# A decoder step with routed experts: where GpSimd's gathers stand among its scatters

## The reference, cut to what matters

```python
rows = jnp.zeros((R, D), x.dtype).at[dest].set(x[tok])        # rows grouped by expert, in blocks
def expert_block(args):
    xb, e = args
    return swiglu(xb, w_g[e], w_u[e], w_d[e])                 # (silu(x Wg) * (x Wu)) Wd, 1024 -> 256 -> 1024
y = y_rows[dest] * gate.reshape(A)[order][:, None]            # weighted
routed = jax.ops.segment_sum(y, tok, num_segments=N)          # and added back to each token's row
```

## Time and profile before

| what | value |
|---|---|
| median of 3 runs | 2397.28 us (2396.0 to 2401.74) |
| the profiled execution, device time | 2394.25 us |
| its span, first to last instruction | 2392.5 us |
| busy share of the span: PE, DVE, ACT, POOL | 92%, 58%, 49%, 37% |
| mean granted clock of TensorE | 0.957 of full |
| expert loop, first to last `part_copied` of a rest | about 1396 to 2338 us |

### The profile page before, as it was taken

The page is one execution under the profiler, slowest core; times in us unless marked ns, Lnnn a source line. Parts: engine busy times, 40 slices in busy tenths (PEclk is TensorE's granted clock), DMA queues, the critical chain, the costliest instruction groups (busy, mean ns, idle before and its releaser), DMA issues. The chain is left out here.

```text
span 2392.5 us, 48606 instructions
## 1 busy us (share of the span) xinstructions
PE 2201.8 (92%) x18304; PEld 1717.5 (72%) x18304; DVE 1376.5 (58%) x2494; ACT 1177.2 (49%) x1931; POOL 892.6 (37%) x1019
## 2 busy tenths in 40 slices
PE   8999899799877799999999899999999999999990
PEld 7566666679866699996546477777777777777760
DVE  4644355422186545543664377777767777777765
ACT  3366433322143333331211167777777777777762
POOL 0133411000042000000244256767666767766653
PEclk9999899899978799999999899999999999999995
DMA  4000332311000555441133389999999999999844
GB/s 153 14 1 1 131 123 103 124 57 45 35 7 2 171 185 177 151 135 64 36 121 123 106 294 313 314 315 309 317 303 309 311 315 309 318 308 315 280 145 168
DMA packets 97313, 419.15 MB, mean 175 GB/s; under 512 B 21782, under 2 KB 29606, under 8 KB 67238
## 3 DMA queue, kind: packets, MB, share of 16 engines
q1 hardware_dynamic: 63494, 320.46, 37.0%
q0 software_dynamic: 33424, 96.15, 15.0%
q10 hardware_dynamic: 288, 1.05, 0.1%
HBM read 374.46 MB, written 63.09 MB: 183 GB/s over the span
## 5 line engine op out<-in xcount | busy, mean ns | idle before, releaser
L2630 DVE TENSOR_TENSOR split<-mix,split 128x2048 fp32r<-128x2048 f32 x140 | 321.5, 2298 | 250.9 <-ACT split L2553 215.7
L2481 PE MATMUL banks<-split 128*128 128x512 f32 x1680 | 403.1, 395 | 0.0
L2481 PEld LDWEIGHTS banks<-split 128*128 128x128 f32 x1680 | 310.5, 188 | 76.7 <-issue 14.1
L2405 POOL DMA_INDIRECT y_rows<-mix x140 | 292.6, 2090 | 162.6 <-ACT mix L2581 113.1
L2553 ACT CAST split<-mix 128x2048 fp32r<-128x2048 f32 x140 | 266.2, 1903 | 0.0
L2388 POOL DMA_INDIRECT hq<-x_rows,mix x136 | 218.6, 1607 | 85.0 <-POOL mix L2380 59.5
L1992 POOL DMA_INDIRECT slot_table<-route x72 | 68.7, 953 | 474.9 <-DVE route L2197 455.7
L2502 PE MATMUL banks<-split 128*128 128x512 f32 x840 | 211.7, 401 | 5.8 <-DVE split L2659 5.8
L1787 PE MATMUL banks<-merge_split 128*128 128x368 f32 x1152 | 203.0, 333 | 2.3 <-DVE merge_split L1850 2.3
L1787 PEld LDWEIGHTS banks<-merge_split 128*128 128x128 f32 x1152 | 196.8, 189 | 2.5 <-DVE merge_split L1850 2.5
L2502 PEld LDWEIGHTS banks<-split 128*128 128x128 f32 x840 | 154.2, 190 | 35.5 <-issue 5.9
(11 more groups left out here) (380 smaller groups left out, 3943.6 us busy)
## 6 DMA issues: line engine op xcount, KB each, us to landing
mix<-in_w_exp_down SPq DMA_DIRECT2D x70, 1024.0 KB
merge_rest<-in_w_merge SPq DMA_DIRECT2D x47, 768.0 KB, 4.3
mla<-in_w_exp_gate SPq DMA_DIRECT2D x35, 1024.0 KB
mla<-in_w_exp_up SPq DMA_DIRECT2D x35, 1024.0 KB
mix<-in_w_exp_gate SPq DMA_DIRECT2D x35, 1024.0 KB
mix<-in_w_exp_up SPq DMA_DIRECT2D x35, 1024.0 KB
inputs_rest<-in_x_tiles SPq DMA_DIRECT2D x9, 512.0 KB, 4.3
mla<-in_x_cols SPq DMA_DIRECT2D x12, 368.0 KB, 10.4
```

What stands on the lines that cost most here:

```text
L2405: pool.indirect_dma_start(out=S.y_dram, in_=y[0:p, s, hf], in_offset=None, compute_op=ALU.add, out_offset=bass.IndirectOffsetOnAxis(ap=si[ ...
L2481: ins = pe.matmul(PS[:, MBANK].rearrange("p (j n) -> p j n", j=2), xr[:, a, k], wr[:, s, GATE:UP + 1, b, DEXP * k:DEXP * (k + 1)], start=( ...
L2630: dve.tensor_tensor(parts(s, j)[:, LO], raw[s][j], parts(s, j)[:, HI].bitcast(F32), ALU.subtract).then_inc(parted[j], 1)
```

## The change

In POOL's step for a block, the call that issues the block's two scatters now stands ahead of the gathers of the third block ahead.

```diff
@@ stage_experts, gpsimd, body @@
                     factors(*ahead(s, it, 2), at[s + 2])
+                scatter(s, it, at[s], first)
                 if s < gathers:
                     pool.wait_ge(xr_full, 2 * (n + 2))
                     pool.sem_inc(passed, 1)
                     gather(*ahead(s, it, 3), at[s + 3])
-                scatter(s, it, at[s], first)
```

## The result

The changed kernel takes 3165.68 us (median of 4 runs, 3162.96 to 3166.49), the one before 2396.64 in the same comparison: 1.32 times as long, 95% interval 1.3173 to 1.3226. That is 769 us more, or 11.48 for each of the 67 blocks whose gathers moved. The forecast was 3034.

The account below looks back on a forecast made before the run. PE was taken as the bound, busy 199.26 of 200 us. Period 13.6 + 7.24 + 2.4 = 23.2 against 13.69: 67 x (23.24 - 13.69) = 640 us, added to 2394.25, gave 3034 us; range 2860 to 3200.

Parts of the forecast that it names:

- each mark named at the end of the prediction: L2449 idle 6 to 7 us until the gather's DMA, period 22 to 24, issue ending T + 11.7, clock under 1.00.
- T: The end of ACT's last copy of a block, which releases POOL; the prediction counts all times in a block from it.
- The landing: Gathered rows land 1.9 us after POOL's issue ends, so PE's turns (transposes of them) start at T + 13.6, not T + 6.4.
- the drain: DMA engines working off a block's 13.0 us of transfers from about T, empty before T + 14, the gather last.
- From the turns to T: PE's transposes of gathered rows, down product, its rest and ACT's copy, up to the next T: 7.24 us at full clock.
- The lower clock: After PE's gap of 7 us, 5.4 us at 1.2 of 2.4 GHz following each restart, costing 2.4 us a block.
- The price by the Trainium skill: Skill page's 1.67 us throttled per tile, half of it lost; gave a period of 21.7 and a total near 2930 us.
- Clock up throughout: Rival: PE's clock stays up or recovers at once despite the gap; 479 us added, 2873 us; chance 0.12.
- Quick POOL: Rival: POOL's calls run quicker once collisions shift; gathers landed at T + 9.0, period 16.2, 2565 us; chance 0.04.
- The rival with the clock down over the whole ring: PE's clock stays low from T through scatter, gather, turns and down to next T; period 25.6, 3192 us; chance 0.12.
- Not slower: Rival: scatters land sooner and free `y` sooner, so POOL, ACT and PE never wait; 3.4 us won, 2391 us; chance 0.02.
- no effect: Rival: the change only rotates POOL's cyclic list of calls; 2394 us; chance 0.02.

Follow-up runs that it names:

- clock held: Changed kernel plus 76 transposes of the identity on PE ahead of its wait for the gathered rows, in every block but the first two: 2990.27 us.
- the run with the short DVE operation: Changed kernel with DVE's subtraction of the gate and up weights cut from 2048 to 256 columns: 3146.88 us.
- light weights besides: Changed kernel with each weight load cut from 2048 to 512 columns and DVE's gate and up subtraction cut to 256: 2964.13 us.
- the kernel with the adds behind and light weights: Changed kernel with only the two scatter DMAs put back behind the gathers and each weight load cut from 2048 to 512 columns: 2547.93 us.

## Why the prediction was right, and where its sizes were off

The mechanism held: each mark named at the end of the prediction showed up, with three sizes beyond it. The wait of L2449 is 8.6 us in the mean and not 6 to 7, the period 25.2 and not 22 to 24, the DMA share 0.51 and not near 0.6.

- **What moves, how often, and POOL's issue.** 67 blocks; scatters from T + 0.9, picks held by DVE's subtraction, issue ending at T + 11.8 against 11.7. As worked out. The factors' new place is free, shown by its own run.
- **The landing** is the term that was mis-sized: 1.9 after the issue, turns at T + 13.6. It measured 3.5 and T + 15.3 early in the loop; over 67 blocks the mean start is T + 15.1. Two reasons. The lower bound came from a scatter that landed 1.35 after its issue, and a gather alone takes 2.7. That scatter was a poor stand-in: its packets in the trace are 23 rows, and the next block's scatter, with 8 rows, took 1.34, where a gather of the loop moves some 130. Nor were the DMA engines idle beside it: the heading of the rows says that no weights are loaded there, but weight packets ran to 2317.9, 0.8 us before its issue ended. No run varied the number of rows. The other reason: the drain was placed right (the windows above are full to T + 14), and no landing was added behind it. 1.5 us x 67 = 100 us.
- **From the turns to T, and the clock.** 7.24 at the full clock: 7.2 with the clock held. The lower clock: 2.4 expected for 5.4 us of it after the restart; 4.7 us of it in the block shown, up to 8.0 in others, and 2.6 by the run that held it. The period's second part is 10.0 in the mean instead of 9.6: 0.4 x 67 = 27 us. With the landing's 100 that is the 132 us between 3034 and 3166, but for 5.
- **The price by the Trainium skill.** Its figure (the Trainium skill, "TensorE: Matmul & The Clock Gate", section "HAM oscillation — how this bites in real kernels") gave an estimate of 0.84 us a block for a cold restart, and a total of 2930. This case does not agree: the clock-held run says 2.6 us a block.
- **The rivals.** Clock up throughout is refuted by the clock row. Quick POOL was made in the run with the short DVE operation: its issue ends at T + 8.9, and the turns still start at T + 15.4, since the drain holds them. With light weights besides, they start at T + 12.2 and not at T + 9.0. The rival with the clock down over the whole ring, 3192, is nearest in time for the wrong reason: the clock came back 4.7 us after the restart in the block shown, before the next T. That the range reached to 3200 was owed to this rival. The forecast with the latest landing that it allowed, T + 14.4, comes to 3088 only, so that the measured 3166 lies in the range is in part luck. Not slower and no effect are refuted by the time.

## What to carry to other kernels

Before moving an issue on an in-order engine, write down which event its new predecessor waits for, and follow it round: if it comes back to the moved transfer's consumer, the period becomes the sum of that ring and every busy share falls. Price a landing from a transfer of its own kind and size, and look at the drain of what shares the engines as a second bound. Where PE gets a gap of several us in each pass, add its lower clock after each restart.

## What the runs showed of the hardware

In the kernel with the adds behind and light weights PE waited 0.8 to 2.8 us in 63 blocks, and in 29 of them the granted clock fell to 0.50 for a stretch after PE was busy again (at 1543.5 us in the rows above, full clock in the gap itself); I had expected that of gaps of 4 us and more. The length of the gap alone did not decide: the clock fell after one of 1.3 us and stayed up after one of 2.4. Of the 26 gaps of 1.6 us and more 18 were followed by it, of the 37 shorter ones 11. A gather of 132 rows of 4 KB landed 2.7 us after its issue on idle DMA engines; scatters of 23 and of 8 rows took 1.35 and 1.34. Issued 3 us after T, beside 3 MB of weight loads, the gather took 5.5 to 7. Transposes of the identity in the gap kept the granted clock at 1.00 for 800 us, where the same kernel without them ran at 0.77.
